# Routed experts: y scaled by its gate and added to the residual in memory each step, in place of stored rows that are gathered at the end

## What is computed

```
def run_block(args):
    tok, e = args
    xb = u_pad[tok]
    hid = jax.nn.silu(xb @ w_g[e]) * (xb @ w_u[e])
    return hid @ w_d[e]
...
yb = yb * row_gate[:, None].astype(yb.dtype)
return jnp.zeros((n + 1, d), yb.dtype).at[row_tok].add(yb)[:n]
...
h = h + hier_moe(rmsnorm(h, p['ln_ffn_g']), p)
return rmsnorm(h, ln_final_g)[:, N_META:]
```

## Time and profile before

| what | value |
|---|---|
| time, median of 3 runs | 1385.98 us (1384.41 to 1387.23) |
| span of the profiled execution, from its first to its last instruction | 1385.8 us |
| busy: PE, PEld, DVE, ACT, POOL | 88%, 73%, 66%, 61%, 15% |
| bytes moved | 312.76 MB, 226 GB/s over the span |
| mixer and router | up to about 646 us |
| plan | 646 to 657 us |
| experts: first list issued, last y out of PSUM | 657.33 us, 1321.2 us |
| combine: first gather, end | 1331.97 us, 1385.8 us |

### The profile page before, as it was taken

One profiled execution on the slowest core, in us unless ns is written; L12 is line 12 of the kernel. 1 busy time (PEld: TensorE's weight loads), 2 busy tenths in 40 slices (PEclk: granted clock), 3 DMA queues, 4 the chain that ended last, 5 costly groups with the idle time before them and its releaser, 6 DMA issues. The chain is left out here.

```text
span 1385.8 us, 22556 instructions
## 1 busy us (share of the span) xinstructions
PE 1215.3 (88%) x5991; PEld 1017.9 (73%) x5991; DVE 921.2 (66%) x1175; ACT 847.0 (61%) x1013; POOL 201.5 (15%) x200
## 2 busy tenths in 40 slices
PE   4999999846999999981699999999999999999910
PEld 3998888835778888871588888888888888888800
DVE  5575555243566666753688876665888888888638
ACT  6438888253666656630678765565777777777412
POOL 1000000022112221111111111101011111111141
PEclk9999999956999999995799999999999999999965
DMA  5210110083233234101899988687999999999758
GB/s 186 82 52 25 38 38 15 22 300 88 79 79 78 78 113 121 46 31 31 353 418 419 420 332 321 242 312 287 385 398 400 405 403 407 399 403 409 267 197 348
DMA packets 73449, 312.76 MB, mean 226 GB/s; under 512 B 15025, under 2 KB 24754, under 8 KB 48834
## 3 DMA queue, kind: packets, MB, share of 16 engines
q1 hardware_dynamic: 52994, 256.12, 48.2%
q0 software_dynamic: 20416, 56.18, 11.6%
HBM read 274.27 MB, written 37.96 MB: 225 GB/s over the span
## 5 line engine op out<-in xcount | busy, mean ns | idle before, releaser
L2011 DVE TENSOR_TENSOR e_lo<-raw,e_hi 128x2048 fp32r<-128x2048 f32 x192 | 432.7, 2288 | 69.8 <-ACT e_hi L1949 64.8
L1949 ACT ACTIVATE e_hi<-raw 128x2048 fp32r<-128x2048 f32 x192 | 356.4, 1912 | 62.2 <-DMA raw<-in_w_gate 43.0
L1838 POOL DMA_INDIRECT ex<-u_dram,ix x37 | 77.8, 2102 | 327.8 <-DMA ix<-list_dram 312.7
L603 PE MATMUL pj<-h_hi,w_hi 128*128 128x432 f32 x336 | 123.8, 368 | 0.1
L1883 PE MATMUL ps_g<-e_hi,ex_hi 128*128 128x512 f32 x288 | 118.2, 411 | 4.0 <-DVE ex_lo L2026 4.0
L603 PE MATMUL pj<-h_lo,w_hi 128*128 128x432 f32 x336 | 121.2, 361 | 0.0
L603 PE MATMUL pj<-h_hi,w_lo 128*128 128x432 f32 x336 | 120.8, 360 | 0.0
L1883 PE MATMUL ps_g<-e_hi,ex_lo 128*128 128x512 f32 x288 | 115.0, 399 | 0.0
L1883 PE MATMUL ps_g<-e_lo,ex_hi 128*128 128x512 f32 x288 | 114.8, 398 | 0.0
L1883 PE MATMUL ps_u<-e_hi,ex_hi 128*128 128x512 f32 x280 | 113.9, 407 | 0.0
L1883 PE MATMUL ps_u<-e_lo,ex_hi 128*128 128x512 f32 x280 | 110.9, 396 | 0.0
(11 more groups left out here) (277 smaller groups left out, 2368.8 us busy)
## 6 DMA issues: line engine op xcount, KB each, us to landing
raw<-in_w_gate SPq DMA_DIRECT2D x64, 1024.0 KB, 10.3
raw<-in_w_up SPq DMA_DIRECT2D x64, 1024.0 KB, 8.0
raw<-in_w_down SPq DMA_DIRECT2D x64, 1024.0 KB
y_dram<-y_sb POOLq DMA_DIRECT2D x35, 512.0 KB
k_win<-k_dram POOLq DMA_DIRECT2D x20, 384.0 KB, 6.5
w_raw<-in_w_in SPq DMA_DIRECT2D x14, 512.0 KB, 3.7
xh<-in_x SPq DMA_DIRECT2D x10, 512.0 KB, 6.9
h_dram<-xh SPq DMA_DIRECT2D x10, 512.0 KB, 2.8
```

What stands on the lines that cost most here:

```text
L603: mm = pe.matmul(ps[:, bank, 0:CH], w[s][:, k, :], h[:, k, cols], start=(k == 0 and n == 0), stop=(k == KD - 1 and n == 2))
L1838: pool.indirect_dma_start(x[s][:, :], None, u_dram, bass.IndirectOffsetOnAxis(ap=ix[s][:, 0:1], axis=0)).then_inc(x_in[s], 16)
L1949: act.activation(w_hi[s][:, :], raw[s][:, :], ACT.Copy).then_inc(hi_done, 1)
L2011: dve.tensor_tensor(w_lo[s][:, :], raw[s][:, :], w_hi[s][:, :].bitcast(F32), ALU.subtract).then_inc(lo_done, 1)
```

## The change

`y_dram`, the slots and `combine` are gone. A list's entry now has two words, the token and its gate. ACT multiplies by the gate while it copies y out of PSUM. POOL adds the 128 rows to `h2_dram` in memory by an indirect transfer with an add (`add_to_h2`). Two blocks can hold the same token, so each add must have landed before the next is issued; SP waits for it (`y_added`) before it loads the next list for y, and it does so ahead of that step's weight loads. Every expert has at least one block, so that the first is expert 0. Lists are filled ahead with row numbers behind the tokens, which `h2_dram` and `u_dram` have 128 of.

There is one loop body a block in place of two. Raw, hi and lo buffers belong to a kind (gate, up, down; two halves each), and there is one buffer for x and one for its list in place of two. The last norm stands at the end of the experts' block, with the residual in the raw buffers. Products, splits and the number of loads are the same.

```diff
-        h2_dram = dram("h2_dram", [REAL, D], F32)
-        u_dram = dram("u_dram", [REAL, D], F32)
+        h2_dram = dram("h2_dram", [ROWS, D], F32)
+        u_dram = dram("u_dram", [ROWS, D], F32)
         k_dram = dram("k_dram", [P, 2, 2, META + P + REAL + P], F32R)
-        y_dram = dram("y_dram", [YROWS, D], F32)
-        list_dram = dram("list_dram", [(EXP + 1) * LIST, 1], I32)
+        list_dram = dram("list_dram", [(EXP + 1) * LIST, 2], I32)
...
-        plan(nc, sem, counts, start, table, table_dram)
...
-        experts(nc, sem, a, ident, iota_e, start, expert1, expert2, place1, place2, slots, table, list_dram,
-                u_dram, h2_dram, y_dram, g_final, z, g_in, z_in)
-        combine(nc, sem, eps_t, gate1, gate2, slots, h2_dram, y_dram, out, g_final, z, g_in, z_in)
...
+        plan(nc, sem, counts, table, table_dram)
+        experts(nc, sem, a, ident, eps_t, table, list_dram, u_dram, h2_dram, out)
...
+        spare_rows = 2 * (EXP + 1) * LIST // P
+        spare = feat[:, 0, 0:spare_rows].bitcast(I32)
...
-            sp.wait_ge(fills, 2)
-            sp.dma_start(list_dram.rearrange("(p c) o -> p (c o)", p=P),
-                         zeros[:, 0:(EXP + 1) * LIST // P].bitcast(I32)).then_inc(fill_dma, 16)
-            sp.dma_start(y_dram[2 * REAL:YROWS, :], zeros).then_inc(fill_dma, 16)
+            sp.wait_ge(fills, 3)
+            sp.dma_start(list_dram.rearrange("(p c) o -> p (c o)", p=P), spare).then_inc(fill_dma, 16)
+            sp.dma_start(h2_dram[REAL:ROWS, :], zeros).then_inc(fill_dma, 16)
+            sp.dma_start(u_dram[REAL:ROWS, :], zeros).then_inc(fill_dma, 16)
...
             pool.memset(xr[:, :, :], 0.0).then_inc(xr_cleared, 1)
+            pool.iota(spare.rearrange("p (r c) -> p r c", c=2), pattern=[[1, spare_rows // 2], [0, 2]], base=0,
+                      channel_multiplier=spare_rows // 2).then_inc(rows_numbered, 1)
...
+            dve.wait_ge(rows_numbered, 1)
+            dve.tensor_single_scalar(spare, spare, P - 1, ALU.bitwise_and).then_inc(rows_masked, 1)
+            dve.wait_ge(rows_masked, 1)
+            dve.tensor_single_scalar(spare, spare, REAL, ALU.add).then_inc(fills, 1)
...
+                for j, gate in enumerate((gate1, gate2)):
+                    pool.tensor_copy(entry[j][s][:, 0:1].bitcast(I32), token[:, bass.ds(b, 1)]).then_inc(token_done, 1)
+                    pool.tensor_copy(entry[j][s][:, 1:2], gate[:, bass.ds(b, 1)]).then_inc(token_done, 1)
+                pool.wait_ge(token_done, 4 * b + 4)
                 take_waits(pool)
                 for j in range(2):
                     pool.indirect_dma_start(list_dram, bass.IndirectOffsetOnAxis(ap=addr[j][s][:, 0:1], axis=0),
-                                            token_s[s][:, 0:1], None).then_inc(listed[s], 16)
+                                            entry[j][s][:, :].bitcast(I32), None).then_inc(listed[s], 16)
...
+        def blocks_less_2(eng):
+            return eng.value_load(table[0:1, 3:4], min_val=EXP - 2, max_val=MOSTBLK - 2)
...
+            def list_of(m, dst, done):
+                at = field(sp, m, 1, EXP * LIST)
+                sp.dma_start(dst[:, :], list_dram[bass.ds(at, P), :]).then_inc(done, 16)
+
+            def load_new(m, weights, k, kind):
+                e, new = field(sp, m, 0, EXP - 1), is_new(sp, m)
+                lo_done, arrived = kind[5], kind[3]
...
-            def step(n, s):
-
-                sp.wait_ge(x_in[s], 8 * (n - s) + 16)
-                lists(n + 2, s)
-                for weights, k, m, s0 in ((a["w_down"], KDN, n, D0), (a["w_up"], KG, n + 1, U0), (a["w_gate"], KG, n + 2, G0)):
-                    e, new = expert(m), is_new(sp, m)
-                    for c in range(2):
-
-                        sp.wait_ge(lo_done, chunk_of(n, s0 + c) + 1)
-                        sp.sem_inc(waited_sp, 1)
-                        with sp.If(new > 0):
-                            load(weights, k, e, c, s0 + c)
-                        with sp.If(new < 1):
-
-                            sp.sem_inc(arrived[s0 + c], 16)
-
-            more = more_pairs(sp)
-            with sp.Fori(0, more + 1) as i:
-                step(2 * i, 0)
-                step(2 * i + 1, 1)
-            odd = one_more(sp)
-            with sp.If(odd > 0):
-                step(2 * more + 2, 0)
...
+                    sp.wait_ge(lo_done, 2 * m - 1 + c)
+                    sp.sem_inc(waited_sp, 1)
+                    with sp.If(new > 0):
+                        load(weights, k, e, c, kind)
+                    with sp.If(new < 1):
+                        sp.sem_inc(arrived[c], 16)
...
+            list_of(0, ix_x, ix_x_in)
+            list_of(0, ix_y, ix_y_in)
...
+            load_new(1, a["w_gate"], KG, gates)
+            load_new(1, a["w_up"], KG, ups)
+
+            most = blocks_less_2(sp)
+
+            sp.wait_ge(x_in, 32)
+            list_of(2, ix_x, ix_x_in)
+            load_new(2, a["w_gate"], KG, gates)
+            load_new(2, a["w_up"], KG, ups)
+            load_new(1, a["w_down"], KDN, downs)
+            with sp.Fori(0, most) as i:
+
+                sp.wait_ge(x_in, 16 * i + 48)
+                list_of(i + 3, ix_x, ix_x_in)
+
+                sp.wait_ge(y_added, 16 * i + 16)
+                list_of(i + 1, ix_y, ix_y_in)
+                load_new(i + 3, a["w_gate"], KG, gates)
+                load_new(i + 3, a["w_up"], KG, ups)
+                load_new(i + 2, a["w_down"], KDN, downs)
+            sp.wait_ge(y_added, 16 * most + 16)
+            list_of(most + 1, ix_y, ix_y_in)
+
+            sp.wait_ge(y_added, 16 * most + 32)
             sp.sem_inc(waited_sp, 1)
+            for b in range(NB):
+                sp.dma_start(z[b], h2_dram[b * P:(b + 1) * P, :]).then_inc(z_in[b], 16)
+            for b in range(NB):
+                sp.wait_ge(normed, b + 1)
+                sp.dma_start(out[b * P:(b + 1) * P, :], z[b]).then_inc(stored, 16)
+            sp.wait_ge(stored, 16 * NB)
...
+            def gather(m):
+                pool.wait_ge(ix_x_in, 16 * m + 16)
+
+                if not isinstance(m, int) or m > 0:
+                    pool.wait_ge(x_turned, m)
...
-            def store(n):
-                at = field(pool, n, 2, 2 * REAL)
-                pool.wait_ge(y_out, n + 2)
-
-                pool.wait_ge(y_stored, 16 * n) if not isinstance(n, int) or n > 0 else None
...
+            def add_to_h2(m):
+                pool.wait_ge(y_out, m + 2)
                 pool.sem_inc(waited, 1)
-                pool.dma_start(y_dram[bass.ds(at, P), :], y[:, :]).then_inc(y_stored, 16)
+                pool.indirect_dma_start(h2_dram, bass.IndirectOffsetOnAxis(ap=ix_y[:, 0:1], axis=0), y[:, :], None,
+                                        compute_op=ALU.add).then_inc(y_added, 16)
...
             for m in range(3):
-                gather(m, m % 2)
-            gather(3, 1)
-            store(0)
-            more = more_pairs(pool)
-            with pool.Fori(0, more) as i:
-                gather(2 * i + 4, 0)
-                store(2 * i + 1)
-                gather(2 * i + 5, 1)
-                store(2 * i + 2)
...
+            most = blocks_less_2(pool)
+            with pool.Fori(0, most) as i:
+                gather(i + 3)
+                add_to_h2(i)
+            for m in range(2):
+                add_to_h2(most + m)
+                pool.wait_ge(y_added, 16 * most + 16 * m + 16)
...
+            with pe.Fori(0, most + 1) as i:
+                gate(i + 1)
+                turn_hid(i)
+                up(i + 1)
+                turn_x(i + 2)
+                down(i)
...
+            def y_from_psum(m):
+                act.wait_ge(d_used, 2 * m + 2)
+                act.wait_ge(ix_y_in, 16 * m + 16)
+                act.activation(y[:, :], ps_y[:, :, :].rearrange("p b c -> p (b c)"), ACT.Copy,
+                               scale=ix_y[:, 1:2].bitcast(F32)).then_inc(y_out, 1)
...
+            with act.Fori(0, most + 1) as i:
+                silu_of(i + 1)
+                hid_split(i)
+                split_new(i + 2, gates)
+                x_split(i + 2)
+                split_new(i + 2, ups)
+                y_from_psum(i)
+                split_new(i + 1, downs)
+            hid_split(most + 1)
+            y_from_psum(most + 1)
...
+            for b in range(NB):
+                act.wait_ge(z_in[b], 16)
+                act.wait_ge(squared, b) if b else None
+                act.activation(square[:, :], z[b], ACT.Square, accum_out=ssq[:, b:b + 1]).then_inc(squared, 1)
+                act.wait_ge(squared, b + 1)
+                act.activation(rms[:, b:b + 1], ssq[:, b:b + 1], ACT.Sqrt, bias=eps_t[:, :], scale=1.0 / D).then_inc(rms_done, 1)
```

More of the change, by code:

```diff
@@ L1575, in _, with plan @@
             run(dve, step)
-PLAN_STEPS = 27
-def plan(nc, sem, counts, start, table, table_dram):
+PLAN_STEPS = 18
+def plan(nc, sem, counts, table, table_dram):
     with ExitStack() as ctx:
@@ L1644, in _ @@
```

(56 more changed lines are left out.)

468 lines of the change are left out of this document (171 added, 297 removed).

## The result

The changed kernel takes 1746.51 us (median of 4 runs, 1744.13 to 1751.22) against 1386.31 us before: a ratio of 1.2605, with an interval of 1.2587 to 1.2623. The forecast was 1652 us, so its direction is right and its loss of 266 us is 94 short. The profiled execution of the changed kernel took 1744.13 us at a span of 1742.3.

A forecast was written before the change was run, and what follows sets the result against it. PE was taken as the bound, transfers close behind; after the change a closed chain, a to e, sums to 28.9 us a step, and with start and end to 1652 us. Range 1510 to 1850, the forecast's own 1560 to 1740.

The forecast's parts named there:

- a: On SP, after an add lands: a field read and a list, then two field reads before the first load; 2.5 us.
- b: Six weight loads on idle DMA engines: the first 4.7 us to landing, five more at 2.5; 17.2 us.
- c: The list for x landing behind the sixth load: between 0 and 2.0 us, taken as 0.5.
- d: POOL's gather instruction, 1.6 us beside VectorE, and 0.3 to the next instruction; 1.9 in the sum.
- e: The add on POOL, from its instruction's start to landing: 6.8 us, ends 3.6 and 12.3.
- T: Time of one routed step, add to add through the closed chain: 28.9 us in place of 18.15.
- The cheap: Rival on POOL's add: it takes 3.6 us, 3.2 less for each of 34 adds, total 1543; chance 0.10.
- the dear add: Rival on POOL's add: it takes 12.3 us, 5.5 x 34 more, total 1839; chance 0.14.
- the Trainium skill's fit: POOL transfer at about 2.0 us plus bytes at 436 GB/s: 3.2 us for 512 KB, whole 1530; no separate chance.
- overtake the loads: Rival in the DMA queue: the list passes the loads, y's path counts, 3.7 x 32 less, total 1534; chance 0.09.
- A low clock: Rival on PE: idling keeps its clock low, a step lasts up to 36.3 us, total 1889; chance 0.04.
- Not slower: Rival on SP: loads stay ahead, a step stays at 18.15 us, only the end counts, total 1356; chance 0.03.

The follow-up runs named there:

- the first experiment: Against the changed kernel, the list for y and the wait for the add's landing move from SP to POOL; 1374.25 us, ratio 0.9926 to the kernel before.
- the list ahead: Against the changed kernel, SP reads the list for x one block further ahead and issues it in front of the six loads; 1680.81 us.

## Why the prediction held, and where its size fell short

The mechanism is shown. One order on SP, wait before loads, closes the chain; taking the wait out of SP brings 1374, moving it behind the loads 1422. Most signs named came as written: PE at 69% with a clock of 0.83, a DMA share of 0.64, SP's longest wait the add, a gather 21.3 us behind the add's landing. Two came out longer: steps around a second block took 24.1 to 27.4 us, not 19 to 24, and the end 30.1, not 28. The stated range holds 1746.5, but the forecast's own, 1560 to 1740, ends 6 us short of it: it allowed for the add alone, and the add was not what was off.

The terms, forecast and measured in the step shown: a 2.5, 2.9; b 17.2, 17.3; c 0.5, 1.1 (0.3 for the list, 0.8 until POOL starts); d 1.9, 2.7; e 6.8, 6.8. **T 28.9, measured 30.9.** The add, the term with the widest bounds, was right, in part by luck: it was put together from a gather's 5.4 and 1.4 of a store, while the plain scatter takes 4.4 and the adding 2.6. The term that failed most there is d, 0.8 of the 1.9 us in the step shown: "VectorE will have less to do, so 1.6". It has less to do in the whole, but the gather comes just when DVE splits (busy 10.00 of 10 us in the stretch 790 to 800), and its median is 2.42 us; that the splits lengthen it is not shown by a run of its own (see the last section).

```profile
L1816 POOL DMA_INDIRECT ex<-u_dram,ix_x x32: 1575/2424/3029, 737.1 to 1664.7; - x32
```

The whole, of the span's 1742.3 against 1651.7, a difference of 90.6 (the median lies 4.2 above that span; an execution's time is itself 1.8 longer than its span, which the prediction put at nothing):
- Up to the first add's landing, 715.9 where 718.9 stood: -3.0. The experts' first list went out at 649.50, 7.5 early, so from there to the landing took 4.5 longer than forecast, and the two errors hide each other. The mixer ended earlier by some 6 us. Up to 3.8 of that is spread between executions: the eight kernels that share this mixer put that list at 649.50 to 653.28. The cause of the rest is open.
- 26 full steps at 2.0: +52.
- Six steps around second blocks, 154.4 in place of 3 x (18.9 + 23.9) = 128.4: +26. Six times the 2.0 of a full step are 12 of it. For the other 14 the prediction took off the loads that are skipped and gave SP no time to skip them.
- The last two blocks, from the landing at 1674.4 to that at 1712.2: 37.8 in place of 25.3, +12.5. SP skips four loads there too, and PE made the last product from rest: "half a product 2.8" was a whole one, 8.3 us, because its other operand's split (hid_lo) came behind the late weights' splits.
- The end, 30.1 for 27.7: +2.4.

These make 89.9. SP's skipping, from the list for y to the first load that is issued (2.06 in a full step), and the last product, from the timeline and a stretch:

```profile
902.28 0.33 SPq L1752 DMA_DIRECT2D ix_y<-list_dram  x1
908.53 1.23 SPq L1748 DMA_DIRECT2D raw_d<-in_w_down  x2
...
1696.04 0.79 PE L1894 MATMUL ps_ey<-d_hi,hid_hi 128*128 128x512 f32 x1 [15.46 <-DVE hid_lo L2018]
...
1704.38 1.11 ACT L1953 ACTIVATE y_sb<-ps_ey,ix_y 128x1024 f32<-128x1024 f32 x1 [10.93 <-PE ps_ey L1894]
...
1696.00:1700.00 4.00, 3.96 (x9) 3.14 (x10) 0.00 (x0) 0.00 (x0) 0.00 (x0) 0.50 0.00 0
```

The rivals. The cheap and the dear add fell by the landing of 7.0, and so did the Trainium skill's fit (DMA: Bandwidth & Descriptors, Anatomy of one DMA — SWDGE (gpsimd) path) as I used it: 3.2 us for 512 KB is less than the 4.4 of the plain scatter and the 7.0 of the add. The list does not overtake the loads: it lands 0.3 behind them, and in front of them the step is 2.1 shorter. A low clock was there (0.83) but did not bind in the full steps, whose ring does not pass through PE; with the wait elsewhere the same products run at 1.00. "Not slower" needed loads that stay ahead of the add, which is what the first experiment gives: 1374, with 1356 forecast for it. There the last copy of y starts 13.7 us later than in the earlier trace rows (1333.86) and the end from there takes 37.2 us in place of 65.6, so the rest of the change is worth having, if only 11 us of 1385.

## What to carry to other kernels

A wait on the engine that issues the loads holds back everything behind it in that program: put it behind the loads (here 1422 us), or on the engine that already orders the work waited for (1374). After opening a chain look for the next ring, for a transfer that took 7 us beside a nearly empty queue takes 11 to 13 beside full loads, and a list that waits for its own buffer can close a ring too. Where a conditional skips a load, the issuing engine still pays for the test.

## What the hardware showed that I had not expected

An indirect add of 512 KB lands 7.0 us after its instruction starts when the queues are nearly empty, 10.8 and 12.6 beside loads; the same scatter without the add takes 4.4.

POOL's gather instruction lasts 0.98 us while DVE is idle (at 789.82 in the kernel with the wait behind the loads, at 780.10 in that with the list ahead) and 2.40 beside DVE's splits (798.80). No run changed this alone. The Trainium skill (SBUF — State Buffer, SBUF: two separate sides) says that VectorE and GpSimd share a pair of ports as an exclusive lock, taken also by a VectorE instruction with two SBUF inputs, against a GpSimd instruction that reads SBUF. DVE's subtract of hi from raw has two such inputs, so the gather's rows agree with it. The splits do not show their half: two take 4.49 us beside that gather (798.06) and 4.48 without one (783.40 in the kernel with the wait behind the loads). The lock itself no run here shows.

Skipping four loads costs SP 4.2 us (6.25 against 2.06 to the first load that is issued), over two thirds of the 6.1 that it takes to issue four (780.40 to 786.53 in the step above).
